# Expert loop of a decoder-layer kernel: the w_down loads move from the sync engine's DMA queue to ScalarE's

## The reference

```python
for e in range(N_EXPERTS):
    hid = jax.nn.silu(h @ w_gate[e]) * (h @ w_up[e])
    y = y + dense_gate[:, e:e + 1] * (hid @ w_down[e])
```

## Time and profile before

| | |
|---|---|
| time, median of 3 runs | 1787.67 us (1786.09 to 1790.24) |
| the profiled execution's own time | 1787.84 us |
| its span, first to last instruction | 1786.1 us |
| granted TensorE clock, mean | 0.945 |
| PE busy | 1603.4 us (90%) |
| DVE / ACT / POOL busy | 528.3 / 200.0 / 94.7 us |
| bytes moved by DMA | 536.94 MB, mean 301 GB/s |
| expert loop (first to last round of PE) | 988.9 to 1751 us |

### The profile page before, as it was taken

How to read it: one execution, slowest core, us unless ns; L and a number is a source line. 1 busy time by engine, 2 the same in 40 slices (tenths; PEclk the granted TensorE clock), 3 DMA queues, 4 the chain that set the end, 5 groups by cost and what they waited for, 6 DMA issues and landing times.

```text
span 1786.1 us, 24827 instructions
## 1 busy us (share of the span) xinstructions
PE 1603.4 (90%) x9535; PEld 913.9 (51%) x9535; DVE 528.3 (30%) x919; ACT 200.0 (11%) x335; POOL 94.7 (5%) x172
## 2 busy tenths in 40 slices
PE   3679999999999999899967999999898988999893
PEld 0036666634777775477744544454443534445351
DVE  0010009631221322542145223232323223232225
ACT  0000001300000002340025000101000000000002
POOL 3000000000110100000001000000000000000000
PEclk7679999999989989899987999999999999999997
DMA  9998888876443445184332999999999999999991
GB/s 350 422 386 333 308 333 306 328 289 237 159 129 97 151 142 186 49 314 142 141 141 107 363 407 415 401 421 421 409 411 404 412 399 411 407 414 414 414 393 61
DMA packets 79389, 536.94 MB, mean 301 GB/s; under 512 B 10385, under 2 KB 10561, under 8 KB 18065
## 3 DMA queue, kind: packets, MB, share of 16 engines
q1 hardware_dynamic: 72146, 507.62, 71.6%
q0 software_dynamic: 6576, 26.35, 4.8%
q10 hardware_dynamic: 624, 2.36, 0.3%
HBM read 533.40 MB, written 11.80 MB: 305 GB/s over the span
## 4 chain that ended last, share of the span: by engine, by line
PE 69%; DMA 19%; DVE 5%; SPq 4%; issue 2%; ACT 2%; ACTq 0%; DVEq 0%
PE ps L589 18%; PE ps L1095 13%; DMA ring<-w_gate 12%; PE ps L933 7%; PE ps L602 6%; PE ps L1115 5%; DMA ring<-w_ada 5%; PE ps L573 4%; SPq L383 3%; PE ps L1077 3%; DMA arena<-w_down 1%; PE ps L1041 1%; PE ps L745 1%; DVE arena L1917 1%; PE ps L1083 1%
## 5 line engine op out<-in xcount | busy, mean ns | idle before, releaser
L1095 PE MATMUL ps<-ring,arena 128*64 128x256 f32 x3200 | 359.4, 383 | 17.9 <-DMA ring<-w_gate 17.9
L589 PE MATMUL ps<-arena,ring 128*128 128x288 f32 x1280 | 321.7, 410 | 0.0
L1095 PEld LDWEIGHTS ps<-ring,arena 128*64 128x64 f32 x3200 | 227.2, 138 | 165.4 <-DMA ring<-w_gate 33.7
L589 PEld LDWEIGHTS ps<-arena,ring 128*128 128x128 f32 x1280 | 240.6, 190 | 89.8 <-issue 25.5
L1115 PE MATMUL ps<-arena 128*64 128x512 f32 x800 | 180.6, 597 | 29.7 <-DMA arena<-w_down 16.7
L573 PE MATMUL ps<-ring,silu_c 128*32 128x512 f32 x768 | 118.3, 727 | 51.2 <-DMA ring<-w_ada 24.6
L1115 PEld LDWEIGHTS ps<-arena 128*64 128x64 f32 x800 | 53.8, 136 | 140.4 <-issue 86.5
L933 PE MATMUL ps<-arena,ring 128*128 128x288 f32 x512 | 124.7, 406 | 0.0
L602 PE MATMUL ps<-ring,arena 128*128 128x512 f32 x256 | 117.2, 606 | 1.3 <-ACT arena L1179 0.7
L1077 PE MATMUL ps<-arena 64*128 64x512 f32 x384 | 104.6, 636 | 12.2 <-DVE arena L1917 10.7
L933 PEld LDWEIGHTS ps<-arena,ring 128*128 128x128 f32 x512 | 97.2, 190 | 26.8
(11 more groups left out here) (432 smaller groups left out, 1214.7 us busy)
## 6 DMA issues: line engine op xcount, KB each, us to landing
ring<-w_gate SPq DMA_DIRECT2D x100, 1024.0 KB, 23.9
ring<-w_up SPq DMA_DIRECT2D x100, 1024.0 KB, 26.3
arena<-w_down SPq DMA_DIRECT2D x100, 1024.0 KB, 27.0
ring<-w_ada SPq DMA_DIRECT2D x96, 1024.0 KB, 8.3
ring<-w_in SPq DMA_DIRECT2D x56, 1024.0 KB, 6.4
ring<-w_o SPq DMA_DIRECT2D x16, 1024.0 KB, 6.5
ring<-cache_k SPq DMA_DIRECT2D x16, 512.0 KB, 3.9
ring<-cache_v SPq DMA_DIRECT2D x16, 512.0 KB, 4.0
```

The lines of the kernel that those rows point to most:

```text
L589: last = mm(ps[:, bank, 0:T], ring[:, slot, P * t:P * (t + 1)], uT[:, t, :], start=(t == 0), stop=(t == KC - 1))
L1095: last = mm(ps[B * s:B * (s + 1), 2 + c // 4, 0:256], xgT[:, 4 * (c % 4) + t, :], ring[:, c, 512 * t + 256 * s:512 * t + 256 * (s + 1)], s ...
```

## The change

SP issues chunks 0 to 7 of each block only. The four `w_down` chunks are issued by ACT, from its own DMA queue, at the head of its loop body for the same block: it reads the expert's number from `plan` itself, waits on the same four values of `moe_used` as SP did, and issues four DMAs of 1 MB. Block 0 is loaded by SP as before. Slots, semaphores, sizes and the order on PE, DVE and POOL stay.

```diff
@@ SP
             with sp.Fori(1, NBLK) as i:
                 with sp.If(i < nblocks):
                     e = sp.value_load(plan[0:1, bass.ds(i, 1)], min_val=0, max_val=NE - 1)
-                    for c in range(MOE_CHUNKS):
+                    for c in range(SLOTS):
                         sp.wait_ge(moe_used, i * MOE_CHUNKS + (c + 1))
                         put_expert(e, c, moe_loaded[c])
@@ ACT
             with act.Fori(0, NBLK) as i:
                 with act.If(i < nblocks):
+                    with act.If(i > 0):
+                        e = act.value_load(plan[0:1, bass.ds(i, 1)], min_val=0, max_val=NE - 1)
+                        for q in range(4):
+                            act.wait_ge(moe_used, i * MOE_CHUNKS + (SLOTS + q + 1))
+                            act.dma_start(mslot[q], w_down[bass.ds(e, 1)].rearrange(
+                                "e f n -> (e f) n")[P * q:P * (q + 1), :]).then_inc(moe_loaded[SLOTS + q], 16)
                     act.wait_ge(moe_used, i * MOE_CHUNKS + (MOE_CHUNKS + 4))
                     act.wait_ge(hid_dve, i + 1)
                     A(hsil, ps[:, 2, 0:256], ACT.Silu).then_inc(sil_act, 1)
```

## The result

The changed kernel takes 1794.74 us in the median of 10 runs (1792.06 to 1798.62), the kernel before 1788.18 us (1786.09 to 1790.24, 10 runs): ratio 1.0039, 95% interval 1.0029 to 1.0048. That is 5.2 to 8.6 us slower, where 6.9 was forecast. The profiled execution took 1794.80 us.

The account below looks back on a forecast made before the run. The prediction took the expert loop to be bound by the DMA engines. The lead's 6.4 us and the first round's 0.5 us made 6.9 us, so 1794.5 us against the median, with a range of 1786 to 1815.

Parts of the forecast that it names:

- The DMA engines are the bound, so nothing can be gained on SP: Expert loop: DMA engines set the pace, SP waits because its queue is full; four fewer issues per round gain 0 us.
- SP's late issue was real: Rival, expert loop: a free SP returns 1.5 to 2.9 us per bound round, 1736 to 1761 us; 0.09 including higher rate.
- One packet for one at the same rate: SP's and ACT's queues: engines alternate packets, half rate each, four w_down chunks take 19.8 us; 1789.5 to 1800 us, chance 0.56.
- Served by arrival: Rival, SP's and ACT's queues: loads are served in order of issue, no measurable change, 1788 to 1791 us; chance 0.18.
- two queues lower the rate: Rival, while both queues load: 365 instead of 422 GB/s gives 1869 us, one third of that loss 1819; chance 0.17.
- The lead: Last round's head: 3.6 gate and up chunks must have landed instead of one, 2.6 more, paid once: 6.4 us.
- The first round: Start of the expert loop: w_down issued later, behind ACT's copy, leaves DMA engines idle 0 to 1.5 us; taken as 0.5.
- ACT at no cost: ACT, each round: register load and four issues take 2 us, hidden in 11.6 us of cover before the Silu; 0 us.
- w_down is never waited for: PE at L1115: last w_down chunk lands 23.3 us behind the head, wanted at 27.4; no wait, 4 us to spare.
- The landing times that I named: ACT's w_down loads: land some 7 us (first) to 21 us (fourth) behind their issue, instead of 27.

Follow-up runs that it names:

- The run with one queue: Kernel before, SP still issuing all 12 chunks but waiting for ACT's two PSUM copies ahead of the four w_down issues: 1789.45 us, ratio 1.0004.
- The last experiment: Changed kernel with ACT's four w_down issues moved behind its Silu: 2074.63 us, ratio 1.1608 to the kernel before.
- the run with two of the four chunks: Changed kernel, but SP also loads w_down chunks 0 and 1 and ACT only chunks 2 and 3: 1791.66 us, ratio 1.0014 to the kernel before.

## Why the prediction was right

*The DMA engines are the bound, so nothing can be gained on SP.* SP's issues became short, as expected, and the loop's DMA share stayed at 1.01 and its rate at 411 GB/s from 1020 to 1722 us. "SP's late issue was real" is out: a free SP returned none of its 27 to 52 us.

*One packet for one at the same rate.* 262 and 249 packets in 9 us at 422 GB/s; with packets of half the size, half the bytes. "Served by arrival" and "two queues lower the rate" are both out. `xT` beside SP's queue was the right neighbour; the gather, whose rate of 365 GB/s I gave 0.17, was not a picture of two plain loads.

*The lead.* The forecast was 2.6 chunks, 6.4 us. In the trace of after, ACT's four loads of the round at 1604.31 us were issued from 1606.50 us, but from 1606 to 1609.6 us only SP's queue moved packets:

```profile
q1 hardware_dynamic: 208, 1.50, 100.1%
```

So w_down starts some 5.6 us behind the head and not 3.4, on an engine that still has SP's packets to move. SP's queue then lands 5.6/2.48 = 2.3 chunks alone and 12.6/4.96 = 2.5 shared, 3.2 must be in at the head, 2.2 more than before: 5.5 us. This term was 0.9 us too large, by the 1 us that I took from issue to first packet. The last round began 7.06 us later than before (1728.96 against 1721.90), of which 1.3 us were there already when the loop began (PE's first L1095 at 990.1 instead of 988.8 us, ahead of all that the change touches but small steps): 5.8 us. The landing times agree with the corrected sum: at the last head three w_gate chunks were in and the fourth landed 1.8 us later (issued 1710.45 us, 20.3 us to landing), some 3.3 chunks where the forecast had 3.6. The forecast placed the loss at the last head; the rounds show it paid at once, in the first round in which the chunks in store did not suffice (35.19 us), and not growing from there on.

*The first round.* 0.5 us was an estimate between 0 and 1.5. The run with one queue has this term alone and measures +0.7 us (-0.9 to +2.3); the change in all rounds and in the last four cost the same, 1794.74 and 1794.84 us. It may be zero. So the mechanism was right, but that 1794.5 came within 0.2 us of the median is luck: the corrected terms give 5.5 to 6.0 us where 6.6 was measured, and the interval of 5.2 to 8.6 holds both sums.

*ACT at no cost.* Four issues of 0.34 us each; the Silu waits for PE as before. Right.

*w_down is never waited for.* Right for the change, with 27.4 - (5.6 + 19.8) = 2 us to spare by the corrected start, not 4; in the two rounds from 1600 us the fourth load landed 22.1 us after its issue at the latest, some 26 us behind the head, which leaves 1.4. The last experiment shows what happens when that is used up.

The landing times that I named, 7 to 21 us, are 8.9 to 22.6.

*Signs that did not come.* PE was to wait for chunks 0, 6 and 7; it never waited for chunk 0 (w_gate). The sum of its waits for data in the loop was to rise by 7 us from some 35; it is 34.5 us (18 waits) where it was 34.6. What grew instead is L1095's busy time, 365.9 against 359.4 us, at a granted clock of 0.98 from 1020 to 1722 us where it was 1.00. Is the lower clock then the cause of the loss? The DMA share of 1.01 in the same stretch and the last head, which follows a wait of 2.59 us for w_up in the round before it, speak against it: a faster PE would have waited longer for the same data. And the run with two of the four chunks has the clock at 1.00 and 36.9 us of waits for w_up, and still costs 0.9 to 4.1 us. No run held the clock fixed.

## What to carry to other kernels

When the DMA engines are busy all the time and several loads wait in the queue, a second queue adds no rate; it changes the order of service, packet for packet, from the order of need to half and half. Before loads are moved to another queue, ask for each stream when it is wanted and what will be in the other queue at that time, the next iteration's prefetch too: a stream that is held up a little owes a lead once, one whose consumer then stands still lets the queues run empty in each round. Whether a cost is paid once or per round can be tested by making the change in the last few iterations alone, and in the first half alone.

None of the variants beats the kernel before, in which one queue serves the 12 chunks in the order in which PE uses them.

## What the runs showed that I had not expected

A load from ACT's queue moved its first packet more than 3 us after its issue (issued 1606.50, none up to 1609.6 us) while SP's queue was full. With SP's queue empty this is about 1 us: in the last block of the run with the issues behind the Silu, ACT issued at 2026.73 us, no queue moved a packet up to 2027.7 us, and ACT's had moved 14 by 2028.0 us. So the 1 us of the prediction is what idle engines show; the longer time was seen only where SP's packets kept them busy.

In the run with the issues behind the Silu, 12 us more delay of an issue turned 6.6 us into 286 us. The variants with earlier issues (ahead of the copies, behind them, or two of the four) cost 0.9 to 12 us in all; here each round pays some 12 us. Where between 2 and 14 us behind the head the edge lies, no run tells.
